# Stick-breaking attention: shifted V load in pieces of 112, 15 and 1 rows, weight copies by turns on two engines, a later turn for finished heads

## The reference

```python
for start in range(0, S, Q_BLOCK):                     # 128 queries at a time
    end = start + Q_BLOCK
    z = einsum('bqhd,bkhd->bhqk', q[:, start:end], k[:, :end]) * scale
    mask = arange(end)[None, :] < (start + arange(Q_BLOCK))[:, None]
    log_1mb = where(mask, log_sigmoid(-z), 0.0)
    suffix = cumsum(log_1mb, axis=3, reverse=True) - log_1mb
    a = where(mask, exp(log_sigmoid(z) + suffix), 0.0)
    outs.append(einsum('bhqk,bkhd->bqhd', a, v[:, :end]))
o = rmsnorm(concatenate(outs, axis=1), g)
```

## Time and profile before

| | |
|---|---|
| Median of 3 runs | 3801.47 us (3798.46 to 3802.99) |
| Profiled execution | 3806.69 us, span 3804.9 us |
| TensorE busy | 3528.4 us (93%) |
| VectorE busy | 2167.3 us (57%) |
| GpSimd busy | 1710.7 us (45%) |
| ScalarE busy | 1202.1 us (32%) |
| Attention, stick-breaking steps of half 1 | 767.8 to 850 us |
| Attention, stick-breaking steps of half 2 | 2549.4 to 2738 us |

### The profile page before, as it was taken

How to read it: one execution, slowest core, us unless ns; L and a number is a source line. 1 busy time by engine, 2 the same in 40 slices (tenths; PEclk the granted TensorE clock), 3 DMA queues, 4 the chain that set the end, 5 groups by cost and what they waited for, 6 DMA issues and landing times.

```text
span 3804.9 us, 52002 instructions
## 1 busy us (share of the span) xinstructions
PE 3528.4 (93%) x22042; PEld 2944.3 (77%) x22042; DVE 2167.3 (57%) x2777; ACT 1202.1 (32%) x1983; POOL 1710.7 (45%) x1248
## 2 busy tenths in 40 slices
PE   7989999979999999999899999958999999999998
PEld 6878878857778787887778888746688787878776
DVE  7754566367364545456765466526777446454545
ACT  2212122257222222223122212327766322222223
POOL 4232433518355555546333323701288436555455
PEclk9999999989999999999999999979999999999999
DMA  3100412534201111103111132342122201111111
GB/s 120 35 29 29 150 64 90 175 104 128 89 23 45 56 45 56 66 34 150 34 36 39 43 135 73 136 166 64 48 85 75 78 29 44 45 56 49 51 67 61
DMA packets 79569, 275.81 MB, mean 72 GB/s; under 512 B 8937, under 2 KB 9193, under 8 KB 76780
## 3 DMA queue, kind: packets, MB, share of 16 engines
q1 hardware_dynamic: 70696, 242.25, 18.8%
q10 hardware_dynamic: 8642, 30.24, 2.1%
HBM read 224.23 MB, written 48.23 MB: 72 GB/s over the span
## 4 chain that ended last, share of the span: by engine, by line
PE 69%; DVE 15%; ACT 5%; POOL 4%; issue 3%; DMA 2%; SPq 1%; POOLq 0%; DVEq 0%; ACTq 0%
PE ps L1413 19%; PE ps L1414 18%; PE ps L1415 18%; PE ps L1419 4%; DVE acc L2109 3%; PE ps L1713 2%; PE ps L1683 2%; DVE tf_lo_p L2108 2%; PE ps L1684 2%; PE ps L1718 2%; DVE af_hi_p L2108 1%; ACT wd_hi L1767 1%; DMA uv_shifted<-v_scr 1%; DVE af_lo_p L2108 1%; PE ps L1488 1%
## 5 line engine op out<-in xcount | busy, mean ns | idle before, releaser
L2693 POOL TENSOR_TENSOR ring_lo<-ring_raw,ring_hi 128x512 fp32r<-128x512 f32 (+1 forms) x356 | 600.1, 1692 | 381.4 <-ACT ring_hi L1767 371.7
L1413 PE MATMUL ps<-a_hi,ring_hi 128*128 128x512 f32 x1472 | 591.7, 402 | 28.9 <-DVE af_hi_p L2108 15.8
L1414 PE MATMUL ps<-a_lo,ring_hi 128*128 128x512 f32 x1472 | 579.0, 393 | 0.0
L1415 PE MATMUL ps<-a_hi,ring_lo 128*128 128x512 f32 x1472 | 578.9, 393 | 0.0
L1413 PEld LDWEIGHTS ps<-a_hi,ring_hi 128*128 128x128 f32 x1472 | 279.6, 190 | 103.5 <-DVE af_hi_p L2108 23.4
L1415 PEld LDWEIGHTS ps<-a_hi,ring_lo 128*128 128x128 f32 x1472 | 279.7, 190 | 60.4
L1414 PEld LDWEIGHTS ps<-a_lo,ring_hi 128*128 128x128 f32 x1472 | 279.9, 190 | 54.7
L2108 DVE TENSOR_TENSOR xres<-xres,ps 128x512 f32<-128x512 f32 x352 | 235.2, 684 | 150.9 <-PE ps L1415 148.9
L1413 PE MATMUL ps<-wd_hi,af_hi 128*128 128x512 f32 x704 | 278.3, 395 | 23.5 <-DVE xres L2108 17.5
L1767 ACT ACTIVATE ring_hi<-ring_raw 128x512 fp32r<-128x512 f32 (+1 forms) x286 | 180.5, 635 | 309.6 <-PE ps L1415 197.4
L1414 PE MATMUL ps<-wd_lo,af_hi 128*128 128x512 f32 x704 | 276.9, 393 | 0.0
(11 more groups left out here) (307 smaller groups left out, 8138.0 us busy)
## 6 DMA issues: line engine op xcount, KB each, us to landing
ring_raw<-w SPq DMA_DIRECT2D x92, 512.0 KB, 3.5
ring_raw<-wgu SPq DMA_DIRECT2D x68, 512.0 KB, 3.7
uq<-q_scr SPq DMA_DIRECT2D x96, 256.0 KB, 4.9
ring_raw<-wd SPq DMA_DIRECT2D x34, 512.0 KB, 3.6
ring_raw<-wo SPq DMA_DIRECT2D x32, 512.0 KB, 4.0
uk<-k_scr SPq DMA_DIRECT2D x6, 2048.0 KB, 10.6
rlf<-wgu SPq DMA_DIRECT2D x20, 512.0 KB, 4.4
xraw<-xt SPq DMA_DIRECT2D x16, 512.0 KB, 7.3
```

The source lines that it names most:

```text
L1413: pe.matmul(o, ah, bh, start=begin and i == 0, stop=False)
L1414: pe.matmul(o, ah, bl, start=False, stop=False)
L1415: last = pe.matmul(o, al, bh, start=False, stop=end and i == len(pairs) - 1)
L2693: tt = lambda o, a, b, op: pool.tensor_tensor(o, a, b, op=op)
```

## The change

Three edits. The copies of stick-breaking groups go by turns: even groups to VectorE, odd ones to ScalarE, for both heads, as the differential units have it. The flip of a finished group of stick-breaking heads comes six steps later instead of three; that of differential heads stays at three. The 127 rows of the shifted load become two DMAs, of 112 and 15 rows; the single row keeps its own, and each has a semaphore of its own.

```diff
--- before.py
+++ after.py
@@
             n, x = st["n"], st["x"]
             m = min(4, n - 4 * g)
             b, si = tbank(), slot(st)
-            on_act = g % 2 == 1 if st["kind"] == "d" else g + st["hh"] > 0
+            on_act = g % 2 == 1
             mark = ("ats_act" if on_act else "ats_dve", hf, x, g)
             emit("transposed", hf, st, g, m, b, si, grab(BK[b]), used.get(("ats", si), []), on_act)
             BK[b].free = [mark]
@@
                 BK[b].free = [("mix_lo", hf, u, g)]
                 settle.append((now[0] + 1, (st["mt"], g), ("mix_lo", hf, u, g)))
                 used["oraw", x, g] = [("flip", hf, u, g)]
-            tail.append((now[0] + 3, flip))
+            tail.append((now[0] + (3 if st["kind"] == "d" else 6), flip))
 
         def attend():
             while "dense2" not in env:
@@
                     pool.memset(UVS[0:1, 0, :], 0.0).then_inc(*up("first_zero", hf))
                     for mark in new("pool", [("first_zero", hf)]):
                         pool.wait_ge(*at(*mark))
-                for mark in new("pool", [(f"ld_v{u % 2}", hf, u), ("ld_before", hf, u, 0), ("ld_before", hf, u, 1)]):
+                for mark in new("pool", [(f"ld_v{u % 2}", hf, u)] + [(f"ld_before{i}", hf, u) for i in range(3)]):
                     pool.wait_ge(*at(*mark))
                 tt(UV[u][:, 0:nt, :], UV[u][:, 0:nt, :], UVS[:, 0:nt, :], ALU.subtract).then_inc(*up("shifted", hf, u))
             elif kind == "o_norm":
@@
                 nt = 8 * hf + 8
                 for mark in new("sp", held):
                     sp.wait_ge(*at(*mark))
-                sp.dma_start(UVS[1:128, 0:nt, :], vsc[u, 0:127, 0:nt, :]).then_inc(*up("ld_before", hf, u, 0, by=16))
-                sp.dma_start(UVS[0:1, 1:nt, :], vsc[u, 127:128, 0:nt - 1, :]).then_inc(*up("ld_before", hf, u, 1, by=16))
+                for i, (p0, p1) in enumerate(((1, 113), (113, 128))):
+                    sp.dma_start(UVS[p0:p1, 0:nt, :], vsc[u, p0 - 1:p1 - 1, 0:nt, :]).then_inc(*up(f"ld_before{i}", hf, u, by=16))
+                sp.dma_start(UVS[0:1, 1:nt, :], vsc[u, 127:128, 0:nt - 1, :]).then_inc(*up("ld_before2", hf, u, by=16))
             elif kind == "load_q":
                 hf, u, c, held = a
                 for mark in new("sp", held):
```

## The result

The changed kernel takes 3752.25 us (median; 3751.09 to 3754.09) against 3802.23 us on the same chip: 50 us less, a ratio of 0.987 with a 95% interval of 0.9853 to 0.9887. Measured once more later (the last experiment) it took 3750.25 against 3805.57, 55 us less, 0.9853 (0.984 to 0.9866). Its profiled execution took 3752.4 us, 54.3 less than the one of before. The forecast was 3739, in a range of 3716 to 3766. So the kernel became faster as forecast, and the forecast of 63 us was 8 to 13 too much.

A forecast was written before the change was run, and what follows sets the result against it. TensorE was busy 93% of the span, but waited at attention's starts because the 127-row load went through one DMA engine. Terms 30 + 5 + 13 + 7 + 11 - 3 = 63 us gave 3739 us, range 3716 to 3766.

The forecast's parts named there:

- V spill of half 2: Start of attention in half 2: with the spill no longer late, ScalarE starts at 2516.1 instead of 2546.1, gain 30 us.
- V spill of half 1: Start of attention in half 1: ScalarE starts at 760.6 instead of 766.06, gain 5 us (0 to 5.5).
- Q tiles of unit 1 and the clock: Half 1: TensorE's 9.0 us wait for these tiles goes, plus 4 us of lower clock, together 13 us (9 to 15).
- Later flip: Stick-breaking steps of half 1: TensorE's 5.5 us wait for normed heads goes, plus 1.5 of clock, 7 us (0 to 7).
- Copies in half 1: Stick-breaking steps of half 1: with the moved copies VectorE becomes the bound, a loss of 3 us (0 to 8).
- Copies in half 2: Stick-breaking steps of half 2: half of TensorE's 21.1 us waiting for copies on ScalarE comes back, gain 11 us.
- the entry for unit 1's shifted load in half 2, gain 0: Half 2: the waits name nobody behind this load but GpSimd itself, so cutting it up gains 0 us.
- A: Rival: load pieces do not help, as 8 MB crowd all engines; only later flip and copies count, 3786 us; chance 0.03.
- B: Rival: in half 2 VectorE's copies behind the scan block TensorE, 115 us if in every step, 3862 us; chance 0.03.
- The sign I gave for a wrong forecast: A wait of TensorE on `ats` from VectorE of more than some 10 us would show the forecast wrong.
- C: Rival: the copies by turns bring 21 us instead of 11, nothing lost in half 1, 3721 us; chance 0.17.
- D: Rival: copies by turns give nothing or take a little, and the V spill still lands late (10 us), 3761 us; chance 0.22.

## Why the prediction was right, and where it was off

- **V spill of half 2, 30 us:** right. ScalarE's wait went from 34.37 to 4.78, 29.6 us. The reading of 28 GB/s at a share of 0.07 as one engine of 16 is borne out by the cut at 113 rows (27 GB/s, 0.08).
- **V spill of half 1, 5 us:** right, 9.93 to 4.76, 5.2 us.
- **Q tiles of unit 1 and the clock, 13 us:** right within 1; steps 1 with the load alone are 83.8 - 71.9 = 11.9 shorter, at a granted clock of 0.95 instead of 0.86. Left out was that the subtraction, now early, falls beside VectorE's scans there too: a scan of 768 keys takes 3.62 us instead of 1.74.
- **Later flip, 7 us:** right alone (steps 1 six shorter, 9.2 by the median), 4.2 on top of the load, nothing clear of noise beside load and copies. By the steps the bounds of 0 and 7 held; I took the upper one, and had not asked whether the wait still decides once VectorE does.
- **Copies in half 1, minus 3 us:** right on top of load and flip, 2.9 longer in the one profile, 4.9 in the other. Alone they make the same steps 2.8 shorter, which fits the condition in the prediction, that VectorE is the bound only once parts 1 and 2 have shortened them. With the subtraction of unit 1 cut down steps 1 are 69.1, so that part of the loss may be the collision in half 1 and not the copies' own time; a difference of 1.5 to 3.5 us is too near the noise there to say.
- **Copies in half 2, plus 11 us:** this term of the sum failed. It gave 4.8 in company. The reasoning for half of the 21 us (three engines at 118 to 162 of 188 us) was even too careful: without a collision they bring up to 12 to 14. What failed is the entry for unit 1's shifted load in half 2, gain 0: I had looked for who waits for its subtraction, and not for what runs beside it. It collides with the scans, and after the change VectorE also holds the copies for which TensorE waits. The rows of before that showed the collision were the subtraction at 2598.22 and the scan of 7.33 us beside it.
- **The sum:** The number came out inside the range because the load makes nearly all of it: by the medians the load brought 48.9 us (48 forecast), load and flip 54.8 (55 forecast), and the copies on top, forecast as 8, nothing clear of noise. By the stretches: 5.2 + 11.9 + 4.2 - 2.9 = 18.4 in half 1, 36.7 in half 2 (396.3 - 359.6), 55 us in the profiles, against 22 + 41 = 63.
- **Rivals:** A fell with the cut at 113 rows and with the load alone. B did not come: the waits on VectorE's copies are 11.1 us in half 2, not 115, as one would expect from the two banks and the slack of two groups. The sign I gave for a wrong forecast, more than some 10 us of such waits, is just reached, but it was a poor sign: the copies alone have 11.4 us of such waits in half 2 and bring 13.6. What differs is the longest one, 3.0 against 1.6 us, with the lower clock behind it. C is refuted: part 3 did not bring 21 us. The outcome lies between the forecast and D. Of D, part 3 did give little, but not for a reason that D named, and its late V spill did not come.

## What to carry to other kernels

Look at the number of rows of each DMA, not only at its bytes: with 127 or 113 rows the transfer moved 27 to 28 GB/s, which is about one engine's share, and held up the whole queue behind it; with 112 and 15 the queue was free again in under 2 us. When two edits touch the same engines, try each on top of the other: the copies were worth 13.6 us alone in half 2, and 4.8 beside the load. Where such a load stands ahead of spills that others wait for, its price is their lateness. Before work is moved to VectorE, look for GpSimd instructions that run beside its two-input instructions, and for what will stand behind them in its order.

## What the runs showed of the hardware that was not expected

A VectorE scan and a GpSimd subtraction, both with two inputs in SBUF, exclude each other for their whole length: 6.16 us instead of 3.08, and 7.33 instead of 3.88. In each case shown the one that starts later ends about its own usual length after the other: the scan of 6.16 us 2.94 us after the subtraction, the subtraction of 6.22 us 4.37 us after the scan that it met first. Either can be the one that is late. In the kernel before the subtraction came first and kept its 4.56 us. With the cut at 113 rows a scan came first (2587.65, 3.88 us), and the subtraction took 7.85 us. With load and flip alone both were late, with the copies still on ScalarE:

```profile
2516.79 7.12 POOL L2693 TENSOR_TENSOR uv<-uv,uv_shifted 128x2048 f32<-128x2048 f32 x1 [29.50 <-DMA uv_shifted<-v_scr]
```

```profile
2522.00 4.86 DVE L2633 TENSOR_TENSOR_SCAN rowa<-rowb,rowa 128x1408 f32<-128x1408 f32 x1
```

A DMA that moves at about one engine's rate also holds the issuing queue: the issue behind the 127 rows took 14.20 to 24.46 us in the four places, and the issues of the load cut at 113 rows held the queue for 11.4 to 28.6 us, against 1.4 to 1.7 us for those of 112, 15 and 1 rows in the changed kernel.
